# HGRN's state keys turned by VectorE and a transfer instead of TensorE, with decays from scans

## The chip, the cores and the metric

The kernel runs on one core of a Trainium2 chip. The metric is the device time of one execution in microseconds (us), taken from the first to the last thing that the core does. TensorE's granted clock in the profiled execution is 0.999 of the full 2.4 GHz.

## What is computed

The model is two blocks one after another. The first has a pooling layer and an HGRN layer, the second two layers of attention beside a gated MLP. The change touches only the HGRN layer: 512 tokens and 16 meta tokens ahead of them, 16 heads of width 128. The kernel works in chunks of 128 tokens where the reference says 64, which computes the same. Cut to what matters:

```
q, fp, i_in, gate = split(h @ w_in); q = silu(q)
f = lb + (1 - lb) * sigmoid(fp);  k = (1 - lb) * sigmoid(-fp)
for each chunk:                        # g = log f, bcum = cumsum(g) in the chunk
    scores = q k^T, each pair (t, s) weighted by exp(bcum[t] - bcum[s]), causal
    o      = scores @ v + (q * exp(bcum)) @ S
    S      = exp(b_end) * S + (k * exp(b_end - bcum))^T @ v
o = rmsnorm(o); return (o * silu(gate)) @ w_out
```

The "state keys" are k * exp(b_end - bcum): each key times the product of the f of all later tokens of its chunk. The product with v contracts over tokens, so the state keys are needed with tokens on the partitions, while the kernel has features there.

## The kernel before, in words

The HGRN stage (about 314 to 880 us) is a row of **parts**. A part makes one pair of heads (x = 0, 1) from the weights w_in in eight **units**: f, f, q, q, i, i, g, g. A unit is 8 blocks of 128 input features times 3 matmuls (high and low halves of the numbers, lines 416 to 418), for f and i in two column groups of 264, for q and g in one of 512. Units alternate between two accumulators, `acc[0]` and `acc[1]`, which VectorE must evict. The order of parts is: first (pair 0), odd (1), even (2), an output projection of 8 short units, odd (3), even (4), output, odd (5), even (6), last (pair 7), and then a tail.

While a part makes pair n, it **processes** pair n - 1: `side()` is called twice per unit on TensorE, VectorE and ScalarE (once in the middle of the unit and once at its end on TensorE), and its call number, the slot, picks a step by `STEP_AT`:

- slots 2, 4, 7, 9: the score groups. At level l the keys and queries are multiplied by decays of blocks of 2^(l-1) tokens: queries on VectorE (L700, L708 for the first), keys by `k_times` on GpSimd (L1111), block decays `tb` by `block_products` on GpSimd (L1101), copies of untouched halves on ScalarE (L781, L786). TensorE makes the score products (L558, L569, L577).
- slot 10, `S_KT`: after level 7 the keys carry the whole decay to the chunk's end. TensorE turns them: per head three 128 x 128 transposes (L625) and one of the 16 meta tokens (L627) into `aux`, and ScalarE copies them to `kt` and `ktm` (L792, L794).
- slot 11, `S_KV`: products of keys and values (L634, L636), states on VectorE (L731, L734).
- slot 12, `S_O`: outputs (L644, L646), squares on ScalarE (L799), the norm on VectorE, which waits for the squares at L741.
- slot 14, `S_ON`: outputs turned, gated and split.

Values already go another way: VectorE turns blocks of 32 x 32 (L2245, L2247) into `vb`, ScalarE writes them to a buffer in HBM (`values_out`, `v_turn`), and SyncE reads them back with the blocks in place (`values_in`, five transfers, L988 and L990).

Weights: SyncE loads chunks of two pieces (1 MB, L909) into two `raw` buffers; a load waits until both pieces of its buffer have been split. ScalarE makes the high part of piece j + 3 at the end of unit j (L407, `b_split`), VectorE the low part in the next unit ahead of its eviction (L2291). Every engine, SyncE's queue too, works strictly in program order. `turn_at` counts the chunks loaded and places `values_in(n)` behind the fourth chunk after pair n's own (the second, for the last pair). If an output projection follows pair n, these four are its two chunks and the first two of the next part.

Lines are those of the kernel before throughout; the order rows of the changed kernel have their own.

## Time and profile before

| | us |
|---|---|
| median of 3 runs (1537.08 to 1537.14) | 1537.09 |
| the profiled execution | 1536.35 |
| its span, first to last instruction | 1534.5 |
| TensorE busy (matmuls) | 1524.0 |
| VectorE busy | 1050.8 |
| ScalarE busy | 577.4 |
| GpSimd busy | 362.6 |

Busy time of an engine is the union of its instructions' spans. For matmuls the ends are modelled and overlap the next one's start, so what one costs is the distance between starts. PE is TensorE, DVE VectorE, ACT ScalarE, POOL GpSimd, SP SyncE; SPq is a queue's issue of a transfer.

### The profile page before, as it was taken

The page shows a single profiled execution, that of the slowest core. Times are in us where ns is not written, and L with a number is a line of the kernel's source. Part 1 is how long each engine was busy: PE and PEld are TensorE (multiplying, and loading weights), DVE is VectorE, ACT ScalarE, POOL GpSimd, SP SyncE. Part 2 cuts the span into 40 slices and gives each one's busy share as a digit, 9 for nine tenths or more (in the row PEclk, how much of TensorE's full clock was granted, in tenths as well). Part 3 has the DMA queues.
Part 4 walks back from the last instruction along what each step waited for, and adds up shares of the span by engine and source line. Part 5 has one row for each costly group of instructions (what it writes and reads, how often), then busy time and mean ns, then how long its engine had stood idle before and what let it go on. Part 6 is the DMA issues. An engine that isn't in the chain of part 4 may idle for free.

```text
span 1534.5 us, 29779 instructions
## 1 busy us (share of the span) xinstructions
PE 1524.0 (99%) x12343; PEld 1365.7 (89%) x12343; DVE 1050.8 (68%) x1750; ACT 577.4 (38%) x1038; POOL 362.6 (24%) x333
## 2 busy tenths in 40 slices
PE   9999999999999999999999999999999999999998
PEld 9999999999998899889898898888888988888887
DVE  6656565765767678676887668779715787797246
ACT  5323222353344244434444445472112246531121
POOL 0000000030422124032332214434430043343510
PEclk9999999999999999999999999999999999999999
DMA  5322322323333334322334233554224335452331
GB/s 172 111 83 86 104 87 83 111 83 101 101 107 89 111 90 135 111 84 93 104 113 139 70 112 114 156 159 145 97 96 138 108 105 150 148 170 84 125 121 55
DMA packets 151859, 170.75 MB, mean 111 GB/s; under 512 B 6348, under 2 KB 122480, under 8 KB 151728
## 3 DMA queue, kind: packets, MB, share of 16 engines
q1 hardware_dynamic: 119728, 138.71, 29.1%
q10 hardware_dynamic: 31920, 29.97, 6.6%
q8 instruction: 98, 1.61, 0.4%
q0 software_dynamic: 80, 0.20, 0.1%
q14 instruction: 33, 0.27, 0.1%
HBM read 151.82 MB, written 17.04 MB: 110 GB/s over the span
## 4 chain that ended last, share of the span: by engine, by line
PE 59%; DVE 1%; issue 0%
PE acc L416 17%; PE acc L417 16%; PE acc L418 16%; PE aux L418 1%; PE aux L416 1%; PE aux L417 1%; PE aux L1421 1%; PE aux L577 1%; PE aux L644 1%; PE aux L646 1%; PE aux L1439 1%; PE aux L1440 0%; PE aux L1464 0%; PE aux L1387 0%; PE aux L636 0%; PE aux L569 0%
## 5 line engine op out<-in xcount | busy, mean ns | idle before, releaser
L416 PE MATMUL acc<-xhis,whi 128*128 128x264 f32 (+2 forms) x1848 | 608.9, 330 | 0.0
L417 PE MATMUL acc<-xlos,whi 128*128 128x264 f32 (+2 forms) x1848 | 602.0, 326 | 0.0
L418 PE MATMUL acc<-xhis,wlo 128*128 128x264 f32 (+2 forms) x1848 | 601.9, 326 | 0.0
L416 PEld LDWEIGHTS acc<-xhis,whi 128*128 128x128 f32 x1848 | 348.0, 188 | 29.5 <-issue 0.3
L418 PEld LDWEIGHTS acc<-xhis,wlo 128*128 128x128 f32 x1848 | 347.9, 188 | 29.3
L417 PEld LDWEIGHTS acc<-xlos,whi 128*128 128x128 f32 x1848 | 348.2, 188 | 27.1 <-issue 0.2
L411 POOL TENSOR_TENSOR wlo<-raw,whi 128x1024 fp32r<-128x1024 f32 x84 | 208.4, 2483 | 364.0 <-DVE whi L2617 364.0
L407 ACT ACTIVATE whi<-raw 128x1024 fp32r<-128x1024 f32 x158 | 164.0, 1048 | 131.7 <-PE acc L418 119.3
L411 DVE TENSOR_TENSOR wlo<-raw,whi 128x1024 fp32r<-128x1024 f32 x81 | 99.8, 1235 | 37.2 <-ACT whi L407 37.0
L2291 DVE TENSOR_TENSOR wlo<-raw,whi 128x1024 fp32r<-128x1024 f32 x77 | 95.0, 1236 | 27.3 <-ACT whi L407 27.1
L2617 DVE CAST whi<-raw 128x1024 fp32r<-128x1024 f32 x84 | 61.3, 733 | 54.0 <-PE acc L418 53.8
L1111 POOL TENSOR_TENSOR kb<-kb,fb 128x264 f32<-128x264 f32 x16 | 17.3, 1099 | 279.9 <-PE aux L558 279.9
L1081 POOL TENSOR_TENSOR xns<-sqs 128x528 f32<-128x528 f32 x1 | 1.4, 1434 | 323.4 <-ACT sqs L1697 323.4
L416 PE MATMUL acc<-zhis,whi 128*128 128x264 f32 x256 | 73.3, 286 | 0.0
L418 PE MATMUL acc<-zhis,wlo 128*128 128x264 f32 x256 | 72.7, 284 | 0.0
L417 PE MATMUL acc<-zlos,whi 128*128 128x264 f32 x256 | 72.6, 284 | 0.0
L2191 DVE TENSOR_TENSOR h<-acc,h 128x528 f32<-128x528 f32 x32 | 22.6, 707 | 38.3 <-PE acc L418 38.3
L416 PEld LDWEIGHTS acc<-zhis,whi 128*128 128x128 f32 x256 | 48.2, 188 | 0.7 <-DVE zlos L2203 0.2
L417 PEld LDWEIGHTS acc<-zlos,whi 128*128 128x128 f32 x256 | 48.3, 189 | 0.0
L418 PEld LDWEIGHTS acc<-zhis,wlo 128*128 128x128 f32 x256 | 48.2, 188 | 0.0
L1894 ACT ACTIVATE pr<-sc,sm 128x257 f32<-128x257 f32 (+1 forms) x64 | 30.5, 478 | 46.2 <-DVE sm L2531 46.1
L2513 DVE TENSOR_SCALAR pr<-pr,sm 128x256 f32<-128x256 f32 (+1 forms) x64 | 41.9, 696 | 1.1
(394 smaller groups left out, 2781.6 us busy)
## 6 DMA issues: line engine op xcount, KB each, us to landing
raw<-in_w_in SPq DMA_DIRECT2D x38, 1024.0 KB, 5.6
raw<-in_hgrn_w_in SPq DMA_DIRECT2D x32, 1024.0 KB, 5.9
raw<-in_pool_w_in SPq DMA_DIRECT2D x15, 1024.0 KB, 5.6
raw<-in_pool_w_out SPq DMA_DIRECT2D x8, 1024.0 KB, 4.9
raw<-in_hgrn_w_out SPq DMA_DIRECT2D x8, 1024.0 KB, 5.1
raw<-in_w_out SPq DMA_DIRECT2D x8, 1024.0 KB, 4.9
v_turn<-vb ACTq DMA_DIRECT2D x8, 544.0 KB, 2.7
raw<-in_pool_w_grp SPq DMA_DIRECT2D x4, 1024.0 KB, 5.1
```

The costliest lines, as they stand in the source:

```text
L407: act.activation(piece(whi, kind, m), raw_view(kind, m), ACT.Copy).then_inc(hi_ready, 1)
L411: dve.tensor_tensor(piece(wlo, kind, m), raw_view(kind, m), piece(whi, kind, m), ALU.subtract).then_inc(lo_ready, 1)
L416: pe.matmul(dst, stat[0], mov[0], start=first, stop=False)
L417: pe.matmul(dst, stat[0], mov[1], start=False, stop=False)
L418: return pe.matmul(dst, stat[1], mov[0], start=False, stop=last)
L577: mm = pe.matmul(dst.rearrange("p (b m) -> p b m", m=m), keys, second_halves(mov, m), start=True, stop=True)
L1111: pool.tensor_tensor(first_halves(dst, m), first_halves(src, m), both[:, :, 1].unsqueeze(2).to_broadcast([P, both.shape[1], m]), ALU.mult)\
L1894: act.activation(pr[z][:, x, lo:], sc[z][:, x, lo:], ACT.Exp, bias=sm[z][:, 0, x:x + 1], accum_out=sm[z][:, 1, x:x + 1])\
L2191: dve.tensor_tensor(halves(h[:, n, :]), acc_all(slot), halves(h[:, n, :]), ALU.add)\
L2291: dve.tensor_tensor(piece(wlo, kind, m), raw_view(kind, m), piece(whi, kind, m), ALU.subtract).then_inc(lo_ready, 1)
L2513: dve.tensor_scalar(pr[z][:, x, lo:2 * P], pr[z][:, x, lo:2 * P], sm[z][:, 2, x:x + 1], None, ALU.mult).then_inc(aprob, 1)
L2617: dve.tensor_copy(piece(whi, kind, M), raw_view(kind, M)).then_inc(hi_ready, 1)
```

## The change

The state keys no longer come out of the score levels and no longer pass TensorE.

- VectorE, at slot 12 of pair n's own part and ahead of the norm step of pair n - 1: `decays(x)` for both heads. A memset puts 1 at each chunk's last token; four scans (the meta tokens and the first three chunks; the fourth is not needed) run backwards over f with a product, so that `snb` holds the decay to the chunk's end.
- GpSimd: one product `snb = kb * snb` over 400 columns per head. The last level's key product (`k_times` of level 7) goes.
- VectorE, behind the part's last unit (behind the third unit of the output projection where one follows): `keys_blocks`, 32 x 32 block turns into `ibs`, the buffer of the values' accumulator output, or into `fbs[0]` for the last pair.
- ScalarE, at unit 1 of the next part: `keys_out`, one transfer to `k_turn` in HBM. SyncE: `keys_in`, five transfers back, placed by `turn_at`. ScalarE, at unit 4: `keys_placed`, two copies of 384 columns to `kt`; the `ib` evictions wait for it.
- TensorE: step S_KT is empty. S_KV waits for `kt_ready` and `kt_landed`.

In the diff, the engines come in the order TensorE (S_KT, S_KV), SyncE (`keys_in`, `turn_at`), GpSimd, ScalarE (`keys_placed`, `keys_out`), VectorE (`decays`, `keys_blocks`):

```diff
-                if s == S_KT:
-                    pe.wait_ge(k_step, k_after(pair, LEVELS, x))
-                    pe.wait_ge(sc_done, read(pair, GROUPS - 1, x) - 2)
-                    for c in range(CH - 1):
-                        pe.transpose(small[:, P * c:P * c + P],
-                                     k1[x][:, META + P * c:META + P * c + P], ident[:, :])
-                    pe.transpose(small[0:META, 3 * P:4 * P], kb[par][x][:, 0:META], ident[:, :])\
-                      .then_inc(kt_full, 1)
...
-                    pe.wait_ge(kt_ready, 4 * pair + 2 * x + 2)
+                    pe.wait_ge(kt_ready, 2 * pair + x + 1)
+                    pe.wait_ge(kt_landed, 80 * pair + 80)
...
+            def keys_in(pair):
+                sp.wait_ge(kd_sent, 16 * pair + 16)
+                if pair == 0:
+                    sp.wait_ge(m_zero, 4)
+                else:
+                    sp.wait_ge(kv_full, 2 * pair)
+                cols = k_turn.rearrange("(a p) x t -> p x a t", a=4)
+                w = 32 * (CH - 1)
+                for b in range(4):
+                    sp.dma_start(kts_of(pair)[32 * b:32 * b + 32, :, :, :], cols[:, :, :, w * b:w * b + w])\
+                      .then_inc(kt_landed, 16)
+                sp.dma_start(ktms[0:META, :, :].rearrange("p x (a j) -> p x a j", a=4), cols[0:META, :, :, 4 * w:4 * w + 32])\
+                  .then_inc(kt_landed, 16)
...
-                    turn_at[count + (2 if part == "last" else 4)] = (values_in, n_pair)
+                    turn_at.setdefault(count + (2 if part == "last" else 4), []).append((values_in, n_pair))
+                    turn_at.setdefault(count + 4, []).append((keys_in, n_pair))
...
-                        for x in range(2):
+                        for x in range(2 if g == 0 else 0):
+                            pool.wait_ge(decay_ready, 2 * pair + x + 1)
+                            pool.tensor_tensor(snb[x][:, 0:KEYS], kb[par][x][:, 0:KEYS], snb[x][:, 0:KEYS], ALU.mult)\
+                                .then_inc(kd_ready, 1)
+                        for x in range(2 if g < GROUPS - 1 else 0):
                             pool.wait_ge(sc_full, scored(pair, g, x))
                             k_times(2 * g + 1, x)
...
+                    if process is not None and j == 4:
+                        keys_placed(process[0])
...
+                    if process is not None and j == 1:
+                        keys_out(process[0])
...
+            def keys_out(pair):
+                act.wait_ge(kd_blocks, 2 * pair + 2)
+                if pair:
+                    act.wait_ge(kt_landed, 80 * pair)
+                act.dma_start(k_turn[:, :, :], kd_of(pair)[:, :, 0:SEQ - P + 32]).then_inc(kd_sent, 16)
...
+                    if slot == 12:
+                        decays(0)
+                        decays(1)
...
+                def decays(x):
+                    dve.wait_ge(f_ready, 2 * pair + x + 1)
+                    dve.wait_ge(k_ready, 1 + 2 * pair + x + 1)
+                    dve.memset(snb[x][:, META - 1:KEYS:P], 1.0)
+                    for c in range(CH):
+                        lo, hi = (META + P * (c - 1), META + P * c) if c else (0, META)
+                        done = dve.tensor_tensor_scan(snb[x][:, lo:hi - 1][:, ::-1], fb[par][x][:, lo + 1:hi][:, ::-1],
+                                                      spare[:, 2:3].to_broadcast([P, hi - lo - 1]), 1.0,
+                                                      ALU.mult, ALU.max)
+                    done.then_inc(decay_ready, 1)
...
                     finish(7)
+                    keys_blocks(0)
+                    keys_blocks(1)
```

The order of SyncE's queue, from pair 2's part over the output projection into pair 3's, before (`v_turn` is the values' buffer, w_out the projection's chunks, w_in a part's):

```order
L909 DMA raw<-in_hgrn_w_out 128x4x512 x2
L909 DMA raw<-in_hgrn_w_in 128x8x256 x2
L988 DMA vts<-v_turn 32x8x128 x4
L990 DMA vtms<-v_turn 16x8x32
L909 DMA raw<-in_hgrn_w_in 128x8x256 x6
```

and in the changed kernel:

```order
L915 DMA raw<-in_hgrn_w_out 128x4x512 x2
L915 DMA raw<-in_hgrn_w_in 128x8x256 x2
L994 DMA vts<-v_turn 32x8x128 x4
L996 DMA vtms<-v_turn 16x8x32
L1008 DMA ibs<-k_turn 32x8x96 x4
L1010 DMA ktms<-k_turn 16x8x32
L915 DMA raw<-in_hgrn_w_in 128x8x256 x6
```

The five key transfers stand between the next part's second and third weight chunk.

ScalarE in pair 3's part, unit 1, of the changed kernel: the first level's copies (L793, L798), the keys' transfer out, and the sigmoids behind which the weight split comes:

```order
L793 ACTIVATE q_second<-q_second 128x128x2
L798 ACTIVATE xns<-kb 128x132x2 x2
L1787 DMA k_turn<-ibs 256x1x416
L1765 ACTIVATE sgb<-snb 128x528
L1766 ACTIVATE snb<-snb 128x528
```

The transfer out that SyncE's key transfers wait for is issued here, in unit 1 of the part. VectorE at slot 12 of a part, before:

```order
L2245 STREAM_TRANSPOSE vb<-ib 128x4x4x32
L2247 STREAM_TRANSPOSE vb<-ib 128x32
L741 TENSOR_SCALAR om<-om 128x8
L744 RECIPROCAL om<-om 128x8
L2291 TENSOR_TENSOR wlo<-raw,whi 128x1024
```

and in the changed kernel (the scans are listed as SCALAR_TENSOR_TENSOR):

```order
L2296 STREAM_TRANSPOSE vb<-ibs 128x4x4x32
L2298 STREAM_TRANSPOSE vb<-ibs 128x32
L2310 MEMSET snb 128x4
L2313 SCALAR_TENSOR_TENSOR snb<-fbs,spare 128x15
L2313 SCALAR_TENSOR_TENSOR snb<-fbs,spare 128x127 x3
L2310 MEMSET snb 128x4
L2313 SCALAR_TENSOR_TENSOR snb<-fbs,spare 128x15
L2313 SCALAR_TENSOR_TENSOR snb<-fbs,spare 128x127 x3
L753 TENSOR_SCALAR om<-om 128x8
L756 RECIPROCAL om<-om 128x8
```

Ten instructions have come between the last value turn and the norm's first step.

## Rows read from the trace of the kernel before

**Rows 1.** Page, part 1: busy us (share of span), instructions.
```profile
PE 1524.0 (99%) x12343; PEld 1365.7 (89%) x12343; DVE 1050.8 (68%) x1750; ACT 577.4 (38%) x1038; POOL 362.6 (24%) x333
```
**Rows 2.** Waits, TensorE, 380 to 900 us: us in total, times, longest.
```profile
PE aux L644 <- DVE st L734: 0.5, 1, 0.5
```
**Rows 3.** Timeline, TensorE, pair 1's part: start us, us, instruction, count.
```profile
421.75 0.29 PE L418 MATMUL acc<-xhis,wlo 128*128 128x264 f32 x1
421.87 0.49 PE L625 MATMUL aux<-ident,xns 128*128 128x128 f32 x3
...
422.87 0.28 PE L417 MATMUL acc<-xlos,whi 128*128 128x264 f32 x1
```
**Rows 4.** Timeline, the tail: VectorE, then TensorE ([idle before]).
```profile
867.31 1.11 DVE L734 SCALAR_TENSOR_TENSOR st<-st,tb,aux 128x128 f32<-128x128 f32 x3
...
867.13 0.49 PE L644 MATMUL aux<-vts,ab 128*128 128x128 f32 x2 [0.49 <-DVE st L734]
```
**Rows 5.** Timeline, VectorE, pair 1's part, slot 12.
```profile
429.50 0.70 DVE L2245 STREAM_TRANSPOSE vb<-ib 128x512 f32<-128x512 f32 x1
430.13 0.17 DVE L2247 STREAM_TRANSPOSE vb<-ib 128x32 f32<-128x32 f32 x1
435.12 0.17 DVE L741 TENSOR_SCALAR om<-om 128x8 f32<-128x8 f32 x1 [4.82 <-ACT sqs L799]
```
**Rows 6.** Groups by form: line, count | busy us, mean ns of one.
```profile
L2568 DVE TENSOR_TENSOR xns<-xns,ug 128x512 f32<-128x512 f32 x8 | 14.6, 1831 | 0.3
...
L734 DVE SCALAR_TENSOR_TENSOR st<-st,tb,aux 128x128 f32<-128x128 f32 x48 | 16.7, 348 | 1.7
```
**Rows 7.** Timeline, first query product and score matmuls: last part, then tail.
```profile
778.10 0.69 DVE L708 TENSOR_TENSOR q_second<-q_second,fb 128x512 f32<-128x512 f32 x1
...
780.45 0.37 PE L558 MATMUL aux<-q_first,kb 128*32 128x64 f32 x11
...
833.73 0.68 DVE L708 TENSOR_TENSOR q_second<-q_second,fb 128x512 f32<-128x512 f32 x1
...
834.98 0.65 PE L558 MATMUL aux<-q_first,kb 128*32 128x64 f32 x32 [0.36 <-issue]
```
**Rows 8.** Timeline, SyncE's queue, pair 1's part (a part behind a part).
```profile
404.79 0.61 SPq L990 DMA_DIRECT2D vtms<-v_turn  x1
411.25 0.39 SPq L909 DMA_DIRECT2D raw<-in_hgrn_w_in  x1
```
**Rows 9.** Timeline, SyncE's queue, during the first output projection.
```profile
508.24 2.75 SPq L988 DMA_DIRECT2D vts<-v_turn  x4
511.03 0.68 SPq L990 DMA_DIRECT2D vtms<-v_turn  x1
518.66 0.38 SPq L909 DMA_DIRECT2D raw<-in_hgrn_w_in  x1
```
**Rows 10.** Timeline, ScalarE, unit 1 of pair 3's part.
```profile
532.84 0.85 ACT L786 ACTIVATE xns<-kb 128x264 f32<-128x264 f32 x2
...
538.58 1.05 ACT L407 ACTIVATE whi<-raw 128x1024 fp32r<-128x1024 f32 x1
...
540.34 0.73 ACT L786 ACTIVATE kb<-xns 128x264 f32<-128x264 f32 x2
```
**Rows 11.** Transfers: what, queue, count, KB each, median us to landing.
```profile
raw<-in_hgrn_w_in SPq DMA_DIRECT2D x32, 1024.0 KB, 5.9
...
v_turn<-vb ACTq DMA_DIRECT2D x8, 544.0 KB, 2.7
...
vts<-v_turn SPq DMA_DIRECT2D x32, 128.0 KB, 5.9
...
vtms<-v_turn SPq DMA_DIRECT2D x8, 16.0 KB, 6.0
```
**Rows 12.** Timeline, TensorE, levels 3 and 4 of pair 2.
```profile
546.76 0.45 PE L577 MATMUL aux<-q_first,xns 128*32 128x16 f32 x32
```
**Rows 13.** Line L909, the weight chunks.
```profile
DMA to landing us min/median/max: 4.8/5.6/10.5
```

78 lines of the change are left out of this document (56 added, 22 removed).

## The prediction

> **What bounds the kernel now.** I read the page's busy times first. TensorE is busy for 1524.0 of 1534.5 us [rows 1]. The list of waits charges it with very little from 380 to 900 us, where the changed stage lies, and its longest single wait there is 0.5 us [rows 2]. The granted clock is 0.999 over the profiled execution, which is the 2.4 GHz level, so no gain waits in the clock. Two things follow. A TensorE instruction that goes away shortens the run by its step from start to start, not by its recorded duration, since matmuls overlap. And work that is moved to VectorE, ScalarE, GpSimd or a queue is free as long as it makes none of TensorE's waits end later. The rest is a search for the places where it does.
>
> **The sum is made against the profiled execution**, 1536.35 us (span 1534.5 and 1.9 around it). The median of the runs shown is 0.74 us higher, so the total of the terms is added to 1537.09.
>
> **Term 1, TensorE's turns go: -6.2 us.** In a part the turning step S_KT stands in the middle of unit ("i", 1). In the timeline, the main matmul before it starts at 421.75, six 128-column turns and two of 16 rows follow, and L417 of the next group starts at 422.87 [rows 3]. That is 1.12 us from the last L418 to that L417; without the step it would be two steps of 0.12 us (421.75 to 421.87 is one), 0.24 us. So 0.88 us goes for each pair of heads. The kernel processes eight pairs, seven of them inside a part: 7 x 0.88 = 6.2 us.
>
> The eighth pair is processed in the tail, and there I count nothing. VectorE goes without a gap from the turned level's scores through two weight splits into the states, which end at 868.42, and TensorE already waits 0.49 us for the first head's states at 867.13 [rows 4]. Neither the splits nor the scores ahead of them wait for a turn by TensorE. The 0.88 us saved before it becomes a longer wait at the same place.
>
> **Term 2, the scans: 0.** Per pair VectorE gets 2 memsets and 8 scans (six of 127 elements, two of 15), at slot 12. VectorE idles there for 4.82 us in front of L741, from 430.30 to 435.12 [rows 5], and so, within 0.03 us, in the other six parts that process a pair. The trace has no scan. The nearest row by shape and by dependence is L734, 128 elements in 348 ns; the slowest two-input row is L2568, 512 elements in 1831 ns, 3.6 ns each, so about 460 ns for 127 [rows 6]. With about 0.1 to 0.2 us for each short one and 0.05 between instructions, the block takes 2.9 us by the first and 3.6 us by the second. I take 2.9, since L734 has the same size. Both fit in 4.82 us even after the 0.88 us by which TensorE's next step may come earlier. The product on GpSimd (400 elements, twice) starts when GpSimd has nothing until the next part, and is needed two units later: even at several us each it is in time.
>
> The Trainium skill, "DVE: opcode table, instruction layouts, handler registers and perf-mode slots", section 6 (Datapath and trigger behaviour), says that the built-in scan runs at half throughput, because its feedback costs a bubble per element. No row here shows a scan. By that rule a scan would lie near the upper price, and the sum would not change.
>
> **Term 3, the block turns of the keys at a part's end: +1.3 us.** They are 2 of 384 columns and 2 of 32, behind the last unit's finish. The same instruction takes 0.70 us for 512 columns and 0.17 for 32, with starts 0.63 apart [rows 5]; scaled, the four take 1.2 us (bounds 1.0, if the width scales fully, and 1.5, four recorded durations added). They stand ahead of L708, the first query product of the next pair's step, for which TensorE's first score matmuls (L558) wait. Where an output projection follows they run behind its third unit, where VectorE idles. Of the other places the last part is the tightest: L708 ends at 778.79 and L558 starts at 780.45 [rows 7], 1.66 us apart. TensorE needs about 0.57 us from the last L708 to the first L558 when it really waits (834.41 to 834.98, with the idle time put down to issue [rows 7], since five semaphore instructions stand between them). So 1.66 - 1.2 - 0.57 leaves -0.1: a cost of 0.1 us. In the tail L708 is already last at 834.41, and the turns push it whole: 1.2 us. Nothing later there can give it back, since TensorE is full.
>
> **Term 4, the queue: +3.4 us.** This is the term that the order tells and the diff hardly does. keys_in puts a wait for kd_sent and five transfers on SyncE's queue, straight behind values_in, and every later weight chunk stands behind it. In a part that follows a part, that is harmless: values_in ends at 405.40 (404.79 + 0.61), the write of the keys has landed by then, five more transfers of that pace end near 409.4, and the next weight chunk is not issued before 411.25 [rows 8].
>
> After an output projection (twice: between pairs 2 and 3 and between pairs 4 and 5) it is not. There values_in runs at 508.24 to 511.71, and the next chunk (pieces 4 and 5) is issued at 518.66 [rows 9]. Now SyncE waits from 511.7 for a transfer that ScalarE issues only in unit 1 of the next part, behind its copies of level 1, at 533.69 (532.84 + 0.85) [rows 10]. The steps: 533.7 + 2.7 to land, as v_turn's eight did [rows 11], is 536.4; five transfers at the pace of 508.24 to 511.71 [rows 9] end at 539.9; the chunk then takes 5.9 us (the median of its kind [rows 11]) and is there at 545.8. ScalarE's split of piece 4 started at 538.58 [rows 10], so it is 7.2 us late. The copies behind it ended at 541.07 (540.34 + 0.73) [rows 10]; now 548.3. TensorE's level 3 and 4 products wait for them and started at 546.76 [rows 12]; with 0.2 us for the semaphore that is 548.5, a stall of 1.7 us. VectorE's split and the eviction of unit 2 end near 548.8, and TensorE needs them only after those products, near 549.7, so they add nothing. Later units: VectorE is some 4 us behind and TensorE 1.7; it catches up in the idle time at slot 12. Twice 1.7 is 3.4 us. Bounds: 2 x 0.6 with the fastest landing of any chunk, 4.8 us [rows 13]; 2 x 3 if VectorE's lag reaches TensorE at the next group too.
>
> **Other edits, 0.** ScalarE loses four copies and its wait for the turns, and gains two copies of 384 columns and one issue of 0.33 us per pair. The copies stand at unit 4, where ScalarE is in time by 1 to 2 us for the ib eviction. GpSimd loses the last key product of a pair.
>
> **The sum:** -6.2 + 1.3 + 3.4 = -1.5 us, 1537.09 - 1.5 = **1535.6 us**. On the profiled execution's scale it is 1534.9.
>
> **Rivals.** (a) The queue block costs nothing. For it: 545.8 is built of four estimates, and if the chunk came 1.7 us earlier at both places there would be no stall. Against it: each estimate is a row. Time: 1535.6 - 3.4 = 1532.2.
>
> (b) The other side: the refill behind keys_in is longer than I count. Each us that the chunk comes later counts twice over the run, because the copies behind the split are the last thing that TensorE waits for. It decides from 2.3 us on: 2 x 2.3 = 4.6 us lifts 1535.6 above 1540.2. The key transfers move rows of 96 floats, 384 bytes, instead of the values' 512. If they ran at half pace, five transfers would need 3.3 us more (an estimate from rows 9, where the issue of five takes 3.5) and the time would be 1535.6 + 6.6 = 1542.2. Against it: the 16-row transfer of values, in 128-byte rows, lands in 6.0 us where the 512-byte ones take 5.9 [rows 11]. The Trainium skill, "DMA: Bandwidth & Descriptors", Specifications, states the rule that speaks for it: below 512 bytes a transfer is done as read-modify-write and falls short of line rate. By that rule the time is the 1542.2 of this rival; rows 11 do not bear it out for 128 bytes, though they time whole transfers and not pieces.
>
> (c) The change does not do what it says: the keys land so late in every part that TensorE waits for them at S_KV in place of the turns. The gain is given back, 1535.6 + 6.2 = 1541.8. In the part of rows 8 the last key transfer is issued by 409.4, and S_KV comes half a unit behind the turns of rows 3, after 424, so they would have to take over 14 us.
>
> **Chances and range.** Forecast 0.55 (its own range 1533.6 to 1537.4), (a) 0.22, (b) 0.14, (c) 0.03, and 0.06 for a small miss in the slacks of term 3 and the scans, as much up as down. 0.2% of 1537.1 is 3.1 us, about what a measurement can tell from no change: faster means under 1534.0, slower over 1540.2. Faster: all of (a) and a little of the forecast, 0.26. Slower: (b), (c) and part of the rest, 0.18. Same: 0.56. The range goes from (a)'s 1532.0 to 1540.5, which leaves out most of (b) and (c).
>
> **What would show it.** TensorE: no transposes in S_KT, and unit ("i", 1) shorter by 0.88 us. VectorE: the wait before L741 down from 4.8 to about 1 to 2 us. SyncE: a wait of some 25 us for k_turn at two places, and behind it a split of piece 4 that starts 7 us late and a TensorE wait of 1.7 us for ScalarE's key copies. Tail: L558 1.2 us later after L708. I am wrong if the two waits are absent or are over 3 us, if a scan takes over 0.6 us, or if TensorE waits at S_KV.

## The result and the profile after

The changed kernel takes 1539.14 us (median of 22 runs, 1537.04 to 1541.73) beside 1536.97 us for the kernel before (22 runs, 1535.94 to 1537.93). The ratio is 1.0012, with a 95% interval of 1.0007 to 1.0018. That is 2.2 us slower where I forecast 1.5 us faster. It lies within the range and within 0.2% of no change, but on the other side of zero. The profiled execution took 1538.84 us, span 1537.0, against 1536.35 and 1534.5.

The page after, parts 1 and 3: busy us (share of the span) and instructions, then packets of the DMA queues. It answers to [rows 1].

```profile
PE 1518.5 (99%) x12279; PEld 1360.3 (89%) x12279; DVE 1080.9 (70%) x1862; ACT 574.9 (37%) x1022; POOL 375.6 (24%) x334
...
DMA packets 163893, 177.46 MB, mean 115 GB/s; under 512 B 16332, under 2 KB 134512, under 8 KB 163760
...
q1 hardware_dynamic: 129584, 141.99, 30.6%
q10 hardware_dynamic: 34096, 33.37, 7.2%
q8 instruction: 98, 1.61, 0.4%
```

TensorE has 64 matmuls fewer and is busy for 5.5 us less, and still the span is 2.5 us longer: it waits more. The waits of TensorE from 300 to 900 us (us in total, times, longest), where the kernel before has one of 0.5 us ([rows 2]) and nothing larger:

```profile
PE aux L597 <- ACT kb L798: 3.3, 2, 1.8
PE acc L432 <- issue: 2.4, 3, 1.0
PE aux L578 <- DVE q_second L720: 1.5, 1, 1.5
PE aux L656 <- DVE st L746: 0.9, 1, 0.9
```

The first is term 4 and the third is term 3. The second is in no term: three times TensorE stood idle in the middle of a unit, for nothing that a semaphore shows. The **lag** of a matmul is its start in the trace after minus its start in the trace before. Where it grows, the change costs time; where it falls, the change gains. The account below gives the steps of the lag in us (an ordinary table; place by the time in the trace after).

```
opening loads, before 12 us                           +0.67   (code identical; runs differ by this much)
the turns of seven pairs, -0.79 to -0.88 each         -6.0
idle "issue" at 469.1, 595.9, 688.9                   +1.00 +1.08 +0.73
levels 3/4 after the output projections, 546 and 684  +1.88 +0.21 +2.11
tail: first score products / after them               +1.10 / -0.4
rest                                                  -0.1
sum                                                   +2.3    (the last matmul: +2.4)
```

**The turns.** Their instructions are gone from the trace, and the lag falls at each of the seven places of [rows 3] by 0.79 to 0.88 us.

**The -0.4 in the tail** is no gain of the moved work. The kernel before has a step of 0.59 us there, put down to issue, in the middle of its score products, and the changed kernel has none at the same products:

```profile
843.40 0.45 PE L577 MATMUL aux<-q_second,xns 128*32 128x16 f32 x29
844.25 0.21 PE L577 MATMUL aux<-q_second,xns 128*32 128x16 f32 x2 [0.40 <-issue]
```

**The queue after an output projection**, pair 3's part. SyncE's queue, then ScalarE, then TensorE (start us, us, instruction, idle before):

```profile
535.97 2.53 SPq L1008 DMA_DIRECT2D ibs<-k_turn  x4
538.54 0.62 SPq L1010 DMA_DIRECT2D ktms<-k_turn  x1
539.29 1.69 SPq L915 DMA_DIRECT2D raw<-in_hgrn_w_in  x2
...
533.12 0.57 ACTq L1787 DMA_DIRECT2D k_turn<-ibs  x1
...
545.93 1.06 ACT L422 ACTIVATE whi<-raw 128x1024 fp32r<-128x1024 f32 x1 [7.44 <-DMA raw<-in_hgrn_w_in]
...
548.47 0.41 PE L597 MATMUL aux<-q_first,xns 128*32 128x16 f32 x29 [1.53 <-ACT kb L798]
```

These rows answer to [rows 9, 10, 12]. The chunk that was issued at 518.66 is issued at 539.29, and the split of piece 4 starts at 545.93, 7.35 us later than in [rows 10]. I had 539.9, 545.8, 7.2, and 548.5 for the products that start at 548.47.

**Scans and norm**, pair 1's part, VectorE. The first pass of [rows 5] holds 4.82 us of idle time; here:

```profile
430.04 0.18 DVE L2313 TENSOR_TENSOR_SCAN snb<-fbs,spare 128x15 f32<-128x15 f32 x1
430.07 0.06 DVE L2310 MEMSET snb<- 128x4 f32 x1
430.14 1.14 DVE L2313 TENSOR_TENSOR_SCAN snb<-fbs,spare 128x127 f32<-128x127 f32 x4
431.12 0.06 DVE L2310 MEMSET snb<- 128x4 f32 x1
431.19 1.82 DVE L2313 TENSOR_TENSOR_SCAN snb<-fbs,spare 128x127 f32<-128x127 f32 x3
434.95 0.17 DVE L753 TENSOR_SCALAR om<-om 128x8 f32<-128x8 f32 x1 [1.94 <-ACT sqs L805]
```

The block takes 2.97 us, the idle time left is 1.94, and the norm starts where it did.

**An idle stretch without a cause**, TensorE in pair 1's part:

```profile
468.97 0.28 PE L433 MATMUL acc<-xhis,wlo 128*128 128x264 f32 x1
...
469.09 0.28 PE L431 MATMUL acc<-xhis,whi 128*128 128x264 f32 x1
...
470.38 0.39 PE L432 MATMUL acc<-xlos,whi 128*128 128x264 f32 x1 [1.00 <-issue]
```

The operands of L432 are those of the matmuls around it. From start to start it takes 1.29 us instead of 0.12. In the trace's list of DMA packets one of 16384 bytes on the instruction queue q8 begins at 467.83 and lasts 1.13 us. From here on the question was what this idle time is.

### The profile page after: what moved, and what is told of

Same layout as the page of the kernel before. It is cut to its first block, busy times and chain, and to the rows that moved or that the text cites. A ratio compares the mean times of both kernels' runs of the same rounds, so it can differ in the third digit from the quotient of the medians.

```text
span 1537.0 us, 29890 instructions
## 1 busy us (share of the span) xinstructions
PE 1518.5 (99%) x12279; PEld 1360.3 (89%) x12279; DVE 1080.9 (70%) x1862; ACT 574.9 (37%) x1022; POOL 375.6 (24%) x334
## 4 chain that ended last, share of the span: by engine, by line
PE 49%; DVE 1%; ACT 0%; issue 0%; ACTq 0%; DVEq 0%
PE acc L431 14%; PE acc L433 14%; PE acc L432 14%; PE aux L433 1%; PE aux L431 1%; PE aux L432 1%; PE aux L1446 1%; PE aux L1464 1%; PE aux L1489 0%; PE aux L1465 0%; PE aux L1412 0%; PE aux L656 0%; PE aux L658 0%; PE aux L597 0%; DVE wlo L2367 0%
## 5 line engine op out<-in xcount | busy, mean ns | idle before, releaser
L432 PE MATMUL acc<-xlos,whi 128*128 128x264 f32 (+2 forms) x1848 | 602.2, 326 | 2.4 <-issue 2.4
L432 PEld LDWEIGHTS acc<-xlos,whi 128*128 128x128 f32 x1848 | 348.2, 188 | 30.2 <-issue 3.1
L432 PE MATMUL acc<-zlos,whi 128*128 128x264 f32 x256 | 72.6, 284 | 0.0
L1132 POOL TENSOR_TENSOR kb<-kb,fbs 128x264 f32<-128x264 f32 x16 | 17.3, 1099 | 178.3 <-PE aux L578 178.3
L432 PEld LDWEIGHTS acc<-zlos,whi 128*128 128x128 f32 x256 | 48.3, 189 | 0.0
L805 ACT ACTIVATE sqs<-aux 128x128 f32<-128x128 f32 x56 | 14.7, 278 | 82.6 <-PE aux L658 82.6
```

What stands on the lines that cost most here:

```text
L432: pe.matmul(dst, stat[0], mov[1], start=False, stop=False)
L1132: pool.tensor_tensor(first_halves(dst, m), first_halves(src, m), both[:, :, 1].unsqueeze(2).to_broadcast([P, both.shape[1], m]), ALU.mult)\
```

## The experiments

I number TensorE's instructions as the trace lists them: weight loads, matmuls and its recorded semaphore instructions. This number is an instruction's **place**. A **burst** is the 256 instructions of the products of two levels (L597, L577 before). Their starts span 1.14 us (467.02 to 468.15 in the changed kernel), so they follow each other every 4.4 ns, where main matmuls with their loads take 60 to 120 ns each. (The 5.2 ns in the recorded expectation for after_place counts the last product's modelled end as well.)

A **stall** is a step from one instruction's start to the next for which no semaphore accounts. Every one over 0.6 us from 390 to 900 us ends at a place that leaves the remainder 193 when it is divided by 256 ("193 modulo 256"), and each time a packet of 16384 bytes on the instruction queue has started some 2.5 us earlier. I read this as TensorE's code arriving in **blocks** of 256 instructions, each fetched by one such packet, with a block beginning at each of these places. The experiments move the places, or take other packets out of the way.

### Moving the code: code_shift and before_shift

```
             for n in range(WARM):
                 pe.matmul(aux[:, n % 2, 0:P], ones_d[:, :], ones_d[:, :], start=True, stop=True)
+            for n in range(24):                     # 32 in before_shift
+                pe.matmul(aux[0:32, n % 2, 0:16], ones_d[:, 0:32], ones_d[:, 0:16], start=True, stop=True)
```

> The changed kernel with 24 small TensorE products (32x16) ahead of everything else, so that each later TensorE instruction lies 48 places further in its stream; all else as it is. In the profile of the changed kernel TensorE stands idle three times in the middle of a unit with nothing that it waits for (1.28, 1.46 and 0.73 us from one start to the next at 469.09, 595.94 and 688.88 us), each time at instruction 193 modulo 256 of its stream, with a 16384-byte instruction packet in flight. Theory A (place in the code): a stall comes where a 256-instruction block begins 2 to 30 places inside a burst of 256 level products, which is over in 1.3 us, sooner than the next block is fetched. After the shift no block begins there: the three stalls are gone, the time falls by 2.3 to 3 us against the changed kernel (about 1536.4, ratio to the kernel before 0.9995 or a bit more). Theory B (the fetch is late because the DMA engines carry the key transfers): stalls stay, near the same times, and the time stays at 1.0012 of the kernel before.

> The kernel before with 32 small TensorE products (32x16) ahead of everything, 64 places of shift, no key transfer at all. Theory A: block beginnings now lie 13, 22 and 23 places inside the bursts of level products at 457.6, 546.8 and 729.6 us, where the kernel before had none: one to three new stalls of 0.5 to 1.4 us there, the time +1 to +3 us (1538 to 1540). Theory B: no stall, time unchanged (within 0.4 us).

Measured: code_shift 1542.48 us, ratio to before 1.0038 (1.0024 to 1.0052); before_shift 1538.20, 1.0010 (1.0001 to 1.0019). **Both expectations were built on the wrong shift.** A product of f32 operands is two matmuls and two loads, so the shift was 96 and 128 places, not 48 and 64; and the products ran in the opening, where they cost 1.7 and 2.2 us themselves:

```profile
6.64 2.20 PE L1141 MATMUL aux<-ones_d 128*32 128x16 f32 x64
```

With the right shift, before_shift has three blocks that begin within 40 places of a burst's start: 10 ahead of the burst at 790.0, 4 inside the one at 605.9 and 36 inside the one at 539.9. None stalls; the packets of the first two had started 3.8 and 1.7 us ahead of their bursts. Its +1.6 us is the opening, so that it lands in theory A's 1538 to 1540 is luck. The kernel before's own step at 843.66 is gone too, and the lag falls there by 0.6 us. In code_shift the three stalls are gone from their places and three others have come, at 460.16, 552.69 and 744.33, again all at 193 modulo 256. Where theory A had 1536.4 us, code_shift took 1542.5. So the place in the code moves the stalls. It does not decide alone: two blocks of code_shift begin 9 and 13 places inside bursts without a stall.

### Taking the key packets away: keys_small

```
-  act.dma_start(k_turn[:, :, :], kd_of(pair)[:, :, 0:SEQ - P + 32])
+  act.dma_start(k_turn[:, :, 0:32], kd_of(pair)[:, :, 0:32])
-  sp.dma_start(kts_of(pair)[32 * b:32 * b + 32, :, :, :], cols[:, :, :, w * b:w * b + w])
+  sp.dma_start(kts_of(pair)[32 * b:32 * b + 1, :, :, 0:32], cols[0:1, :, :, 0:32])
...  (the fifth read, of the meta tokens, is cut to one row in the same way)
```

> The changed kernel with the key transfers cut to a token: the write takes 32 columns and each of the five reads one row of 32 columns, the same instructions and waits on every engine. The keys that ScalarE places are therefore wrong: what is left out is the transfer of the keys. TensorE's stream is unchanged. Theory A (place in the code): all three stalls stay, the time falls only by what the shorter landing gives the weights after the output projections (0 to 1 us). Theory B (DMA load delays the fetch): the stalls at 469 and 596, where key packets are under way, go, and the one at 689, where the DMA engines are idle, stays: -2 to -2.5 us.

Measured: 1535.4 us, ratio 0.9989 (0.9980 to 0.9999), 3.7 us under the changed kernel; this kernel leaves out the transfer of the keys. The stall at 469 is gone, those at 593 and 684 stay. That is neither theory: A had all three staying, B had 593 going as well, and the time falls by more than either said. The block is the same, 15 places inside the burst, but its packet starts 1.1 us ahead of the burst (465.25 before 466.39) instead of 0.8 behind it (467.83 after 467.02). The waits for the key copies go down too, from 4.2 us of added lag to under 1, because the smaller transfers let weight chunk 2 be issued at 536.96 instead of 539.29 and its split start at 542.83 instead of 545.93. So this kernel says two things at once, which the next ones separate.

### Moving the key reads in SyncE's queue: keys_later

```
-   turn_at.setdefault(count + 4, []).append((keys_in, n_pair))
+   turn_at.setdefault(count + (6 if n_pair in (2, 4) else 4), []).append((keys_in, n_pair))
```

> The changed kernel with the key reads of the two pairs that an output projection follows put two weight chunks later in SyncE's queue (behind chunks 2 and 3 of the next odd part, ahead of nothing that the odd part needs early). If the two waits of TensorE for ScalarE's copy of the keys (1.5 to 1.8 us in the row, 2.1 and 2.1 us of added lag) come from weight chunk 2 standing behind the wait for the keys' write, both go: -3.8 to -4.5 us against the changed kernel. The rival: the copies are late because ScalarE itself has the key write's wait and issue ahead of them; then the waits stay and the time too. The stalls at 469 and 596 stay by both; the one at 689 may shrink.

Measured: **1533.22 us, ratio 0.9979 (0.9970 to 0.9988)**, 3.4 us under its own runs of the kernel before and 5.9 under the median of the changed kernel. The expectation was -3.8 to -4.5. SyncE's queue now shows both chunks ahead of the keys:

```profile
518.32 18.65 SPq L915 DMA_DIRECT2D raw<-in_hgrn_w_in  x2
537.07 2.71 SPq L1008 DMA_DIRECT2D ibs<-k_turn  x4
```

Both waits for ScalarE's copies are gone: the lag falls by 1.6 to 1.9 us at 546 and by 2.0 at 682. The stall at 689 is gone too. Its block still begins 27 places inside the burst (29 before), but TensorE no longer waits ahead of that burst, and the packet starts 1.9 us ahead of it instead of 1.2 behind. The stalls at 469 and 594 stay, as both theories had it.

### Code place without a price: after_place, before_place

```
                         level_products(pe, 2 * g, par, x)
+                        if pair == 0 and g == 2 and x == 1:
+                            level_products(pe, 2 * g, par, x, 13)   # its first 13 again; 20 in before_place
```

> The changed kernel with 13 of pair 0's level-4 products computed twice (the same values into the same places), inside its third burst of products: 52 more TensorE instructions ahead of pair 1, some 0.3 us by the burst's 5.2 ns for one. Every stall found so far (eleven, in four kernels) sits at instruction 193 modulo 256 of TensorE's stream, one block behind a block that begins between 7 places ahead of a burst of level products and 29 places inside it. Theory A (place in the code is needed): with 52 places of shift no block of pairs 1 to 7 begins there, and the three stalls at 469, 596 and 689 us are gone: 1536.2 to 1537.5, some 2 to 2.5 us under the changed kernel. Theory B (DMA load alone): the stalls stay, the time is 0.3 us longer.

> The kernel before with 20 of pair 0's level-4 products computed twice, 80 more TensorE instructions ahead of pair 1, some 0.4 us. Blocks now begin 3 places ahead of the burst at 457.6 us, 6 places inside the one at 546.8 and 7 inside the one at 729.6. Theory A: up to three stalls of 0.5 to 1.8 us where there were none, without any key transfer: 1538.5 to 1541. Theory B (only late fetches stall, and they are late only beside key transfers): 1537.0 to 1537.4, no stall.

(The count of stalls on record, eleven, should read ten.) Measured: after_place 1542.28 us, ratio 1.0036 (1.0022 to 1.0050), against my expectation of 1536.2 to 1537.5. The three stalls are gone from their places. At 469 and 596 the lag falls by 1.3 and 1.2 us for that, of which 0.4 and 0.3 come back within 20 us. But a block that began 23 places **ahead** of the burst at 684.4 stalled, in the middle of the burst, for 2.57 us. TensorE had just waited 2.1 us there for ScalarE's copies. The windows of TensorE's busy time and granted clock (columns: stretch, length, busy us and count of PE, PEld, DVE, ACT and POOL, then PEclk, the granted clock as a share of 2.4 GHz, DMA share, GB/s) show what that cost besides:

```profile
684.00:688.00 4.00, 1.17 (x115) 1.12 (x116) 3.23 (x6) 1.90 (x4) 0.90 (x1) 1.00 0.03 8
688.00:692.00 4.00, 3.87 (x30) 3.84 (x30) 4.00 (x9) 2.87 (x7) 3.47 (x7) 0.59 0.71 195
688.74:692.15 3.41, 3.41 (x18) 3.41 (x17) 3.41 (x8) 3.02 (x7) 3.41 (x7) 0.50 0.87 245
```

In the 4 us after the stall the granted clock is 0.59 on average. That is a stretch at 0.50, the 1.2 GHz level, from 688.74 to 692.15, and the 2.4 GHz level around it. Against best (below), which has the same places and no stall there, the lag grows by another 1.5 us in it.

before_place took 1538.38 us, ratio 1.0012 (1.0003 to 1.0021), and has **two stalls without any key transfer**, 1.75 us at 460.08 and 0.75 at 734.13, where the blocks begin 3 places ahead of a burst and 7 inside one. The third, 6 inside, did not stall; its packet had started 2.3 us ahead of the burst. The time lies just under theory A's 1538.5 to 1541 and above theory B's 1537.0 to 1537.4. Theory B in its strict form, that only key transfers make a fetch late, is refuted by the two stalls. The waits of TensorE, 300 to 1000 us:

```profile
PE aux L580 <- issue: 1.6, 1, 1.6
...
PE acc L416 <- issue: 0.4, 1, 0.4
```

### The last pair's block turns, and all repairs: tail_keys, best

```
    if s == S_VT:
+       last_keys()          # keys_blocks(0), keys_blocks(1) of the last pair, no longer in finish_pair()
...  (GpSimd: +  pool.wait_ge(kd_ready, 2 * pair + x + 1) ahead of the first level's k_times)
```

tail_keys is keys_later with this; best has after_place's 13 repeated products besides.

> Keys read later in SyncE's queue as before (the changed kernel with that took 1533.2), and the last pair's key block turns behind its first query products on VectorE instead of ahead of them (GpSimd waits for its own key product ahead of the first level, which costs it nothing). TensorE's wait for the second query product (1.5 us at 836 in the changed kernel, 0.4 before) shrinks to 0.2 to 0.5: -1.0 to -1.2 us, so about 1532.1. The rival: ScalarE's key write, which now comes 1.2 us later, delays its copies for the levels 1 and 2, and TensorE waits there instead: no gain.

> Keys later in SyncE's queue, the last pair's block turns behind its query products, and the 13 repeated products of pair 0. Theory A: no stall at 468.6 and 593.6 either: 1530.0 to 1531.5, and a spread between runs of under 1.5 us. Theory B: as without the repeated products, 1532.1 to 1532.5.

Measured: tail_keys 1532.35 us, ratio 0.9973 (0.9963 to 0.9982); **best 1531.52 us, ratio 0.9969 (0.9958 to 0.9980)**, range 1530.78 to 1532.88. The tail of the changed kernel and of tail_keys:

```profile
836.45 0.68 DVE L720 TENSOR_TENSOR q_second<-q_second,fbs 128x512 f32<-128x512 f32 x1
...
837.70 0.65 PE L578 MATMUL aux<-q_first,kb 128*32 128x64 f32 x32 [1.46 <-DVE q_second L720]
```

```profile
829.26 0.69 DVE L720 TENSOR_TENSOR q_second<-q_second,fbs 128x512 f32<-128x512 f32 x1
...
829.86 0.57 DVE L2323 STREAM_TRANSPOSE fbs<-snb 128x384 f32<-128x384 f32 x1
...
830.52 0.65 PE L578 MATMUL aux<-q_first,kb 128*32 128x64 f32 x32 [0.36 <-issue]
```

The wait is back at the 0.36 us of [rows 7], the lag there falls by 1.08 us, and ScalarE's later key write delays nothing. best has no step over 0.6 us at 193 modulo 256. From tail_keys to best the lag falls by 0.1 us at 469 and 0.9 at 594, and the repeated products take 0.2 to 0.3; at 846 it rises by 0.5 again, since best has a step of 0.42 us of its own at such a place there. The medians are 0.8 us apart, but the two kernels' runs overlap (1531.62 to 1533.91 and 1530.78 to 1532.88), so this last gain is not clear of noise, and the spread of 2.1 us is more than the 1.5 that I expected. Against the kernel before all three, keys_later, tail_keys and best, are clear of it. What is left of TensorE's waits from 300 to 900 us:

```profile
PE aux L661 <- DVE st L751: 0.9, 1, 0.9
PE aux L592 <- DVE ab L705: 0.7, 2, 0.4
PE aux L578 <- issue: 0.4, 1, 0.4
PE aux L651 <- DVE ab L701: 0.3, 1, 0.3
PE aux L600 <- issue: 0.2, 1, 0.2
```

best and after_place have the same repeated products. The block that stalled after_place for 2.57 us begins 25 places ahead of the same burst in best, where TensorE comes to the burst without a wait: packet 4.2 us ahead of it, no stall.

### The old places with the new transfers: after_turns, turns_small

```
+                if s == S_KT:
+                    pe.wait_ge(sc_done, read(pair, GROUPS - 1, x) - 2)
+                    for c in range(CH - 1):
+                        pe.transpose(small[:, P * c:P * c + P], ident[:, :], ident[:, :])
+                    pe.transpose(small[0:META, 3 * P:4 * P], ident[:, 0:META], ident[:, :])
```

turns_small is after_turns with keys_small's edit.

> The changed kernel with eight TensorE turns per pair kept where they were (of a constant, the result is read by nobody): the same work and the same number of TensorE instructions as in the kernel before, so each block of 256 begins where it began there, while the key transfers and all the rest of the change stay. My sum says that the turns cost 0.86 to 0.88 us in each of seven pairs, +6.0. Theory A (place in the code): with the old places the stalls at 469, 596 and 689 (3.5 us from start to start, 2.8 of added lag) are gone, so +3.2 against the changed kernel, 1542.3 (range 1541.5 to 1543). Theory B (DMA load alone): the stalls stay, +6.0, 1545. Both waits behind the output projections stay by either.

> The changed kernel with eight TensorE turns per pair kept (of a constant, read by nobody) and the key transfers cut to a token (32 columns; the keys are wrong, their transfer is what is left out). The kernel with the turns and the full transfers had blocks at the old places and stalled all the same, at 469.18 and 751.59, where the kernel before does not; there the instruction packet started at 469.30 and 750.39, when the last of the 384-byte key packets were through, and in the kernel before at 466.18 and 738.47, when the value packets were through. If the key packets are what the fetch stands behind, both stalls are gone, packets start 1 us or more ahead of those bursts, and the time falls by 6 to 9 us from 1545.1 (stalls 2.67 and 1.22, the slower clock after the first 1.5, and most of the two waits behind the output projections 3.5 to 4.4): 1537 to 1539. If the stalls come from the waits that hold TensorE's sequencer, they stay.

Measured: after_turns 1545.08 us, ratio 1.0058 (1.0044 to 1.0072); turns_small 1539.10, ratio 1.0015 (1.0006 to 1.0024). after_turns has every block where the kernel before has it. The stalls at 594 and 689 are gone. At 469 and 752 two blocks that are harmless in the kernel before now stall: 2.67 us at 469.18 and 1.22 at 751.59. Neither theory has this: A had no stall at the old places, B had all three staying, and of those only the one at 469 did, longer than before. That the time is B's 1545 is luck: the new stall and a lower clock make up for the two that are gone. With the key packets cut, in turns_small, the two blocks are harmless again, and its time is at the upper end of the 1537 to 1539 expected. This is the clean test of the load: TensorE has the same code at the same places in both, and the packet starts at 469.30 in after_turns and at 465.62 in turns_small (466.18 in the kernel before). TensorE itself comes to the burst only 0.65 us earlier in turns_small (467.43 and 468.08), so some 3 us of the difference are the packet's own delay. Executions differ, too: keys_later and tail_keys have the same TensorE code and the same transfers up to there, and their packets start 1.22 us behind and 0.12 ahead of that burst, with steps of 1.55 and 0.55 us. The profiled execution of after_turns was the slowest of its five (1548.5); its clock after the longer stall (columns as above):

```profile
468.00:471.00 3.00, 1.36 (x128) 1.20 (x128) 2.90 (x6) 0.80 (x2) 0.72 (x1) 1.00 0.41 83
471.00:476.00 5.00, 4.15 (x23) 4.05 (x23) 5.00 (x11) 3.35 (x8) 3.89 (x8) 0.71 0.70 215
```

And DMA packets of two single microseconds: 466 to 467 in the kernel before, then 469 to 470 in after_turns. The instruction packet comes when the queue q1 is running dry; in after_turns that is 3 us later, and 225 small packets still share the microsecond with it. (The last 384-byte key packets are through only at 471.44, and at 752.85 behind the other stall, not at the packets' starts as the expectation for turns_small says.)

```profile
q8 instruction: 1, 0.02, 7.0%
q1 hardware_dynamic: 48, 0.02, 6.6%
```

```profile
q1 hardware_dynamic: 225, 0.07, 28.1%
q8 instruction: 1, 0.02, 7.2%
```

### Are the scans free: scans_twice

```
-                    for c in range(CH):
+                    for c in [*range(CH), *range(CH)]:
...  (a semaphore, decay_half, between the two passes)
```

> The best kernel so far (1531.5) with all eight scans of a pair run twice by VectorE (the same values again). In the changed kernel VectorE still stands idle 1.94 us ahead of the norm's first step (L753) behind the scans, 4.8 without them. A second pass of some 3.0 us uses that up and makes the norm 1.0 to 1.2 us late in seven pairs. If the scans are free because of that idle time alone, this shows as an idle time of 0 and either no time (the norm itself has slack before TensorE) or up to 7 x 1.1 = 7.7 us. The sum's view, that the norm's result is needed much later: 0 to +0.5 us, 1531.5 to 1532.0. The rival, that the norm's step stands on TensorE's path: 1536 to 1539.

Measured: 1534.49 us, ratio 0.9987 (0.9978 to 0.9996), 3.0 us over best, between the two ranges of the expectation. In the seven parts the second pass costs TensorE nothing: against best the lag stays within 0.3 us up to 839, although VectorE has no idle time left and the norm starts some 0.4 us later:

```profile
432.24 2.98 DVE L2325 TENSOR_TENSOR_SCAN snb<-fbs,spare 128x127 f32<-128x127 f32 x7
435.14 0.14 DVE L759 TENSOR_SCALAR om<-om 128x8 f32<-128x8 f32 x1
```

The time was lost in the tail. The profiled execution (1536.63, one of the slower ones) is 5.7 us behind best's there. VectorE waited for a transfer of the outputs, TensorE 1.3 us for VectorE, and then followed a stall of 2.34 us at 193 modulo 256 and a granted clock of 0.55 (timeline of VectorE, then the window of 6 us, columns as above). The lower clock alone added 2.5 us:

```profile
837.76 3.87 DVE L776 SCALAR_TENSOR_TENSOR sqs<-vb,vec,gb 128x128 f32<-128x128 f32 x8 [2.54 <-DMA vb<-o_turn]
```

```profile
850.00:856.00 6.00, 6.00 (x24) 4.88 (x19) 4.00 (x8) 2.09 (x4) 2.71 (x5) 0.55 0.01 3
```

So the scans are free for TensorE in the seven parts. That the used-up idle time in the last part is what led to the wait in the tail is not shown: the transfer landed 10.9 us after its issue, where the slowest of its kind took 6.9 in best, and I did not pursue why. The clock is not peculiar to this execution: the seven runs with a granted clock of 0.997 took 1533.76 to 1536.98 us, the three with 0.999 took 1533.05 to 1533.24.

### The changed kernel again: after_again

> The changed kernel itself, for a second profile and times on the same chip. The three stalls sit at instruction 193 modulo 256 again, at 469, 596 and 689 us, each 2.4 to 2.7 us behind the start of an instruction packet; their length may differ by 1 us. If one exceeds some 2.3 us, the granted clock is 0.5 to 0.7 in the microseconds behind it, as in two other kernels, which gives part of the spread of 4.7 us between runs. Median 1538.5 to 1540.

Measured: 1538.33 us, ratio 1.0014 (1.0004 to 1.0023). The stalls are at the same three instructions, 0.83, 2.10 and 0.69 us long where they were 1.28, 1.46 and 0.73. The time is just under the expected 1538.5, and one stall ends 3.17 us behind its packet's start, outside the 2.4 to 2.7 expected. None of the three exceeds 2.3 us, and the clock stays at 1.00, so the part of the expectation on the clock was not tested by them. A plain wait of 2.43 us, for ScalarE's copies at 682.6, left the clock at 1.00 as well. The clock of each run is on record, though: the five runs with 0.999 took 1537.01 to 1538.33 us, the four slowest, with 0.997 and 0.998, 1539.75 to 1541.04. In the first series the slowest run of all, 1541.73, has the lowest clock, 0.996, while 0.998 and 0.999 differ by only 0.3 us on average.

### All stalls in one table

Every step of TensorE over 0.6 us that ends at a place of 193 modulo 256, from all fourteen traces (390 to 900 us). There is none in the kernel before, best, before_shift and turns_small. Three shorter steps end at such places as well: 0.59 us in the kernel before (at 843.66, in the tail), 0.55 in tail_keys (at 468.79) and 0.42 in best (at 846.07); there is no other over 0.4.

```
kernel        place   step us   packet starts   from packet to the next instruction
after          8641    1.28        467.83           2.55
after         11457    1.46        594.99           2.41
after         13505    0.73        687.09           2.52
after_again    8641    0.83        466.69           2.51
after_again   11457    2.10        593.13           3.17
after_again   13505    0.69        686.02           2.49
keys_small    11457    1.53        592.03           2.27
keys_small    13505    1.00        682.12           2.78
keys_later     8641    1.55        467.78           2.40
keys_later    11457    1.82        592.98           2.43
tail_keys     11457    1.72        592.18           2.25
code_shift     8385    1.61        459.58           2.19
code_shift    10433    1.12        551.36           2.44
code_shift    15041    1.41        743.21           2.53
after_place   13505    2.57        685.45           2.68
before_place   8385    1.75        459.60           2.24
before_place  14785    0.75        732.32           2.56
after_turns    8641    2.67        469.30           2.55
after_turns   15041    1.22        750.39           2.42
scans_twice   17857    2.34        847.45           2.35
```

TensorE resumes 2.2 to 2.8 us (once 3.2) after the packet starts. It runs 256 instructions in some 15 to 30 us in main matmuls and in as little as 1.4 us when a burst lies in the block. So the fetch was late where (1) a block begins near the start of a burst, 24 places ahead to 29 inside it in these traces, and (2) its successor's packet starts no earlier than about the burst. These two are not enough by themselves: in tail_keys a packet starts 0.4 us behind the start of a burst (681.23 and 680.82) whose block begins 27 places inside, TensorE reaches the next block 2.4 us after the packet's start, and nothing stalls. What decides is whether TensorE gets there sooner than those 2.2 to 2.8 us. The second has at least two causes here: other packets ahead of it (the value reads, and now the key reads, at 469 and 751), and a wait that holds TensorE just ahead of the burst (at 689 and in after_place). For the stalls at 460, 594 and 734, where there is neither a key read nor a recorded wait at the burst, I did not find what sets the packet's time.

The Trainium skill, "Runtime: NRT & Kernel Launch", section "Instruction fetch mechanics", says that an engine's code is refilled in 16 KiB blocks of 256 instructions through a DMA queue of its own. The traces agree (16384-byte packets; places 256 apart). The same section of the Trainium skill calls the cost mostly hidden, since instructions are issued more slowly than they are fetched. Here, at 4.4 ns for an instruction in a burst, it is not: 0.7 to 2.7 us.

## Why the prediction was wrong, point by point

**Term 1 was right.** -6.2 forecast, -6.0 measured. In the tail nothing is left of the eighth pair's turns, as forecast: TensorE's wait for the states grows from 0.5 to 0.9 us.

**Term 2 was right.** 2.9 us per pair forecast, 2.97 measured, and the norm starts on time.

**Term 3 was right.** +1.3 forecast. The tail shows +1.10 at the first score products, and tail_keys takes 1.08 away. The 0.1 us of the last part did not show.

**Term 4 had the right mechanism and was too small.** Each row of its chain came true within 0.6 us, down to the start at 548.47. What I mis-sized is the term: +3.4 forecast, +4.2 measured (1.88, 0.21 and 2.11), keys_later takes back 1.6 to 1.9 and 2.0. At the first place the part as a whole ran 0.17 us earlier than before (L798 at 532.67 where L786 stood at 532.84) and the wait ended where I had it, so it cost 1.88 and not 1.7. The next group added 0.21, where the forecast had nothing. At the second place TensorE and the chain both came 1.2 us later than before, and the chain itself was 0.2 us longer than at the first. The 0.2 us for the semaphore stood in no row; the copies' end at 548.23 and the products' start at 548.47 make it 0.24. Rival (a), that the queue costs nothing, is refuted.

**The step that failed is the sentence "A TensorE instruction that goes away shortens the run by its step".** It took TensorE's stream to be only time. It is also code, which arrives in blocks, and 16 instructions fewer per pair move every later block in it. The sum had no term for that, nor for the instruction queue among those that the key reads pass: +2.8 us in the profiled execution, three stalls that the kernel before does not have. The experiments show both parts of it: at other places all three are gone (after_place, with the load as it was), without the key packets the one at 469 is gone (keys_small, with the places as they were), and without the wait ahead of its burst the one at 689 is gone (keys_later). With +0.8 in term 4, +0.2 in term 1, +0.67 in the opening (noise between executions) and -0.6 in the tail, where 1.1 - 0.4 stands for the 1.3 forecast, this makes 3.9 of the 4.0 us between -1.5 and +2.5. The -0.4 is luck of the same kind: the kernel before's step of 0.59 us at 843.66 is also at 193 modulo 256, and the change moved the code away from it.

**Rival (b)** named longer refills through 384-byte rows. The five key transfers were issued in 3.2 us (535.97 to 539.16), where the values' five took 3.5 [rows 9], and the weight chunk behind them had landed 6.6 us after its issue at the latest (539.29 to 545.93), so the rival's 3.3 us are not there. In the list of packets a 384-byte one takes 22 ns in the median and a 512-byte one 39. **Rival (c)** did not happen: TensorE waits 0.3 us at S_KV, once, for scores and not for keys. The other side was reached by a mechanism that I had not listed.

**What would show it:** the transposes are gone, the wait ahead of the norm is 1.94 us, SyncE waits 24.5 and 24.3 us for k_turn (48.8 in all), the split is 7.35 us late, the tail is 1.1 us late. All of that came true, and the time still moved the other way.

## What to carry to other kernels

After an edit to an engine that issues short instructions at a high rate, look for idle time put down to issue at places a fixed number of instructions apart: there the code itself is late. An edit that moves the code by a few dozen instructions changes the time by some us in either direction: code_shift and after_place came out 3 us slower than the changed kernel (1.7 us of code_shift's in the opening), and best's 0.8 us over tail_keys is not clear of noise. Taking small packets and waits out of the code's way was the surer repair here. Where a transfer sets the end of a wait, price the wait in the part's own time, since the transfer's issue and the waiting engine's arrival both move with all that happened before. And put a wait for a late producer into a queue behind the loads that the consumer needs first: moving two entries of SyncE's queue turned +2.2 us into -3.4.

## What the runs showed of the hardware that I had not expected

- TensorE's code comes in 16384-byte packets, one for 256 of its instructions, and TensorE goes on 2.2 to 2.8 us after such a packet starts. Near a burst of instructions 4.4 ns apart this showed as 20 stalls of 0.7 to 2.7 us.
- The packet queues with data. With the same TensorE code it started 3.7 us later (469.30 against 465.62, 0.65 of it TensorE's own lateness) when full key transfers lay ahead of it. This is one profiled execution of each; two executions with the same load differed by 1.3 us.
- The longest stalls cost twice. Around idle steps of 2.57, 2.67 and 2.34 us the granted clock went to 0.50, the 1.2 GHz level (means of 0.59, 0.71 and 0.55 over the next 4 to 6 us), and it did so in after_turns at a plain wait of 2.38 us for ScalarE too. The cost was 1.5 to 2.5 us each time. After a plain wait of 2.43 us in after_again, and in the other traces with stalls up to 2.10 us, it stayed at 1.00, so the length of the pause alone does not decide in these traces. Part of the spread between runs goes with it: the slowest runs of after_again, after_place, after_turns and scans_twice all have granted clocks of 0.996 or 0.997.
- A product of f32 operands is four TensorE instructions (24 products: 48 matmuls and 48 loads), which matters when instructions are counted.
